# Half the columns in a triangular inverse, and a key norm moved beside the value tiles

## The reference, cut to what matters

```python
qkv = silu(causal_dwconv(concat([q, k, v]), conv_w))
q = l2norm(to_chunks(q)) * D ** -0.5
k = l2norm(to_chunks(k))
...
k_beta = k * beta[..., None]
lower = where(strict, einsum('bhncd,bhnsd->bhncs', k_beta, k) * decay, 0.0)
rhs = concatenate([v * beta[..., None], k_beta * exp(g)[..., None]], axis=-1)
sol = triangular_solve(lower, rhs, left_side=True, lower=True, unit_diagonal=True)
...
# then a scan over chunks: v_new, o_i, state
```

## Time and profile before

| | |
|---|---|
| median of 3 runs | 3832.85 us (3829.78 to 3834.25) |
| the profiled execution | 3828.58 us, span 3826.8 us |
| granted TensorE clock, mean | 0.949 |
| PE busy | 3475.4 us, 91% of the span |
| DVE / ACT / POOL busy | 47% / 34% / 11% |
| matmul L3373, L3385, L3390 | 960, 768 and 960 records |

### The profile page before, as it was taken

The page is one execution under the profiler, slowest core; times in us unless marked ns, Lnnn a source line. Parts: engine busy times, 40 slices in busy tenths (PEclk is TensorE's granted clock), DMA queues, the critical chain, the costliest instruction groups (busy, mean ns, idle before and its releaser), DMA issues. The chain is left out here.

```text
span 3826.8 us, 46458 instructions
## 1 busy us (share of the span) xinstructions
PE 3475.4 (91%) x19317; PEld 2705.3 (71%) x19317; DVE 1780.1 (47%) x2762; ACT 1308.2 (34%) x2038; POOL 420.6 (11%) x351
## 2 busy tenths in 40 slices
PE   5989897999999789998897988999989988899998
PEld 4877765788777567886665756788766665577886
DVE  4775465443332534332544454444444444554534
ACT  2332353223232332322422353333333134533333
POOL 0001000120000101100023000221001310013100
PEclk7999998999999899999899999999989989999999
DMA  6651215333221032331301103232122020213231
GB/s 228 199 175 45 78 34 187 118 124 110 90 75 55 1 132 69 105 109 35 99 18 27 37 1 110 87 100 101 66 76 61 2 63 1 88 55 110 77 110 50
DMA packets 230575, 316.69 MB, mean 83 GB/s; under 512 B 13133, under 2 KB 167606, under 8 KB 229086
## 3 DMA queue, kind: packets, MB, share of 16 engines
q1 hardware_dynamic: 230366, 313.72, 24.9%
HBM read 311.04 MB, written 6.85 MB: 83 GB/s over the span
## 5 line engine op out<-in xcount | busy, mean ns | idle before, releaser
L493 PE MATMUL out<-h_lo,w_hi 128*128 128x512 f32 x2608 | 1043.1, 400 | 52.1 <-DVE w_lo L484 47.8
L494 PE MATMUL out<-h_hi,w_hi 128*128 128x512 f32 x2608 | 1022.2, 392 | 0.0
L495 PE MATMUL out<-h_hi,w_lo 128*128 128x512 f32 x2608 | 1021.6, 392 | 0.0
L484 DVE TENSOR_TENSOR w_lo<-ring,w_hi 128x1024 fp32r<-128x1024 f32 (+2 forms) x459 | 560.7, 1227 | 980.0 <-ACT w_hi L479 974.9
L479 ACT ACTIVATE w_hi<-ring 128x1024 fp32r<-128x1024 f32 (+2 forms) x459 | 469.2, 1027 | 1152.9 <-PE out L495 1061.1
L493 PEld LDWEIGHTS out<-h_lo,w_hi 128*128 128x128 f32 x2608 | 494.0, 189 | 178.1 <-issue 60.4
L494 PEld LDWEIGHTS out<-h_hi,w_hi 128*128 128x128 f32 x2608 | 493.8, 189 | 111.9 <-issue 11.0
L495 PEld LDWEIGHTS out<-h_hi,w_lo 128*128 128x128 f32 x2608 | 493.6, 189 | 103.9
L493 PE MATMUL item_banks<-h_lo,w_hi 128*128 128x512 f32 (+1 forms) x632 | 289.4, 458 | 14.3 <-DVE w_lo L484 5.1
L494 PE MATMUL item_banks<-h_hi,w_hi 128*128 128x512 f32 (+1 forms) x632 | 255.1, 404 | 0.0
L495 PE MATMUL item_banks<-h_hi,w_lo 128*128 128x512 f32 (+1 forms) x632 | 254.8, 403 | 0.0
(11 more groups left out here) (499 smaller groups left out, 4635.8 us busy)
## 6 DMA issues: line engine op xcount, KB each, us to landing
ring<-in_mlp_w SPq DMA_DIRECT2D x30, 2048.0 KB, 8.5
ring<-in_w_up SPq DMA_DIRECT2D x44, 1024.0 KB, 7.4
tiles<-in_mod_w SPq DMA_DIRECT2D x80, 512.0 KB, 4.6
ring<-in_e_w_in SPq DMA_DIRECT2D x48, 512.0 KB, 4.1
ring<-in_w_down SPq DMA_DIRECT2D x10, 2048.0 KB, 7.7
ring<-in_w_in SPq DMA_DIRECT2D x16, 1024.0 KB, 5.2
ring<-in_o_w_in SPq DMA_DIRECT2D x7, 2048.0 KB, 7.9
tiles<-in_mod_w SPq DMA_DIRECT2D x8, 1024.0 KB, 8.8
```

Of the source, the lines that this page charges most:

```text
L484: return nc.vector.tensor_tensor(lo.bitcast(F32R), x, hi, ALU.subtract)
L493: nc.tensor.matmul(out, wh, xl, start=start, stop=False, **kw)
L494: nc.tensor.matmul(out, wh, xh, start=False, stop=False, **kw)
L495: return nc.tensor.matmul(out, wl, xh, start=False, stop=stop, **kw)
```

## The change

**Inverse.** At level n the multiplies L3373, L3385 and L3390 take as moving operand only the columns that the level changes, 32 for each head in place of 64, read in runs of 2<<n (2, 4, 8, 16, 32) columns with as many skipped. The number of matmuls and their stationary operands stay (64x64 each). ACT copies 128x96 in place of 128x192 and writes them in such runs; DVE subtracts 128x192 in place of 128x384 (last level 128x96 in place of 128x192). The copy of each level gets a tile of its own (`y_levels`, 128x1920) that POOL clears once at the start of the lane, since half of its columns are never written and serve as zeros in the stationary operand. To make room, the tiles `sb_q`, `sb_k` and `sb_v` are allocated in the attention region that uses them.

**Order.** The key norm begins at plan 67.9, 3.5 after the last key tile, and is 15.5 long, so that it stands beside the three value tiles. The SiLUs of the value tiles move behind it (plan 84.2, 84.9, 85.6), which keeps the key norm's activation tables loaded. `DELTA` becomes 87.5. Since an item that begins at or after `DELTA` is 9.4 long, item 15 is now one of those; items end at plan 167.6 in place of 163.8, and the rotary lane begins 3.8 later.

```diff
@@ delta_lane
-    v_beta, k_beta, k_end, q_run, run, attn_t, y_sb = pieces(0, 7)
+    v_beta, k_beta, k_end, q_run, run, attn_t = pieces(0, 6)
+    y_sb = [y_levels[:, n, :] for n in range(LEVELS)]
+    HALF = T * HD // 2
+    def part_of(x, n, side):
+        return x.rearrange("p (q two j) -> p q two j", two=2, j=2 << n)[:, :, side, :]
+    def inverses(n, b):
+        size = 2 << n
+        both = scratch(9, 2, 2 * size).rearrange("p (w s) -> p w s", w=2)[:, :, b * T * HD:(b + 1) * T * HD]
+        return both.rearrange("p w (q two j) -> p w q two j", two=2, j=size)[:, :, :, 0, :]
         nc.gpsimd.memset(state[:, :, :], 0.0).then_inc(zeroed, 1)
+        nc.gpsimd.memset(y_levels[:, :, :], 0.0).then_inc(zeroed, 1)
-        pe.wait_ge(zeroed, 1)
+        pe.wait_ge(zeroed, 2)
-                            last = nc.tensor.matmul((B0, B1)[b][at, t * HD:(t + 1) * HD], of_head(parts[n], b, t)[at, :],
-                                                    of_head(inv, b, t)[at, :], start=True, stop=True)
+                            last = nc.tensor.matmul((B0, B1)[b][at, t * HD // 2:(t + 1) * HD // 2], of_head(parts[n], b, t)[at, :],
+                                                    part_of(of_head(inv, b, t)[at, :], n, 0), start=True, stop=True)
-                                nc.tensor.matmul((B2, B3)[b][at, t * HD:(t + 1) * HD], of_head(inv_t, b, t)[at, :], of_head(y_sb, b, t)[at, :],
-                                                 start=True, stop=True)
+                                nc.tensor.matmul((B2, B3)[b][at, t * HD // 2:(t + 1) * HD // 2], of_head(inv_t, b, t)[at, :],
+                                                 part_of(of_head(y_sb[n], b, t)[at, :], n, 0), start=True, stop=True)
-                            last = nc.tensor.matmul((B2, B3)[b][at, (T + t) * HD:(T + t + 1) * HD], of_head(y_sb, b, t)[at, :],
-                                                    of_head(inv_t, b, t)[at, :], start=True, stop=True)
+                            last = nc.tensor.matmul((B2, B3)[b][at, HALF + t * HD // 2:HALF + (t + 1) * HD // 2], of_head(y_sb[n], b, t)[at, :],
+                                                    part_of(of_head(inv_t, b, t)[at, :], n, 1), start=True, stop=True)
-                    nc.scalar.activation(y_sb[:, b * T * HD:(b + 1) * T * HD], (B0, B1)[b][:, 0:T * HD], ACT.Copy).then_inc(y_out, 1)
+                    nc.scalar.activation(part_of(y_sb[n][:, b * T * HD:(b + 1) * T * HD], n, 0),
+                                         (B0, B1)[b][:, 0:HALF].rearrange("p (q j) -> p q j", j=2 << n), ACT.Copy).then_inc(y_out, 1)
-                        nc.vector.tensor_tensor(here, here, (B2, B3)[b][:, 0:N].rearrange("p (w n) -> p w n", w=2), ALU.subtract).then_inc(inv_done, 1)
+                        here = inverses(n, b)
+                        change = (B2, B3)[b][:, 0:2 * HALF].rearrange("p (w q j) -> p w q j", w=2, j=2 << n)
+                        nc.vector.tensor_tensor(here, here, change, ALU.subtract).then_inc(inv_done, 1)
@@ items_lane, scalar
-                steps += [(end, 2, m), (end + 3.0, 3, m)]
+                steps += [(end, 2, m), (end + 3.0 if item.silu_at is None else item.silu_at, 3, m)]
@@ second_mixer
-        BEGIN, DELTA, ROUND = 18.0, 94.0, 28.0
+        BEGIN, DELTA, ROUND = 18.0, 87.5, 28.0
+        keys_end, conv_end = (items[TC + n * GDN_T - 1].begin + items[TC + n * GDN_T - 1].length for n in (2, 3))
+        for t in range(GDN_T):
+            items[TC + 2 * GDN_T + t].silu_at = conv_end + 3.0 + 0.7 * t
-            normed = key_norm_lane(k, r, r.lane(conv_end + 3.5, 9.0),
+            normed = key_norm_lane(k, r, r.lane(keys_end + 3.5, 15.5),
```

More of the change, by code:

```diff
@@ L626, in __init__ @@
         self.chunks, self.scale, self.tile, self.func, self.moving, self.ready, self.each = chunks, scale, tile, func, moving, ready, each
-        self.begin, self.length = 0.0, 0.0
+        self.begin, self.length, self.silu_at = 0.0, 0.0, None
 def left(freed, m):
@@ L3052, in head_norm_lane, with attention_region @@
     return gate_done
-def attention_region(k, a, l, tiles, nq, kc2, vc2, ks2, kw2, vs_rows, vw_rows, gates, sq, sk, sv_rows, gz, mixT):
+def attention_region(k, a, l, tiles, nq, kc2, vc2, ks2, kw2, vs_rows, vw_rows, gates, gz, mixT):
     nc = k.nc
@@ L3068, in attention_region @@
         kc_dup, vc_rows = r.sbuf("kc_dup", [P, 2 * N_CMP]), r.sbuf("vc_rows", [P, 2, HD])
+        sq, sk, sv_rows = r.sbuf("sb_q", [P, SB_T, S]), r.sbuf("sb_k", [P, SB_T, S]), r.sbuf("sb_v", [P, TC, N_SB * HD])
         ranges = [[(W_SQ + t * P, P)] for t in range(2 * SB_T)] + [[(W_SV + t * P, P)] for t in range(2)]
@@ L3465, in _ @@
                         act.wait_ge(t_done, c * 2 * LEVELS)
-                    nc.scalar.activation(y_sb[:, b * T * HD:(b + 1) * T * HD], (B0, B1)[b][:, 0:T * HD], ACT.Copy).then_inc(y_out, 1)
+                    if n == 0 and b == 0 and c == 0:
+                        act.wait_ge(zeroed, 2)
+                    nc.scalar.activation(part_of(y_sb[n][:, b * T * HD:(b + 1) * T * HD], n, 0),
+                                         (B0, B1)[b][:, 0:HALF].rearrange("p (q j) -> p q j", j=2 << n), ACT.Copy).then_inc(y_out, 1)
             yield t0 + 21.0
@@ L3522, in _ @@
                     if n < LEVELS - 1:
-                        here = invs.rearrange("p (w b n) -> p w b n", w=2, b=2)[:, :, b, :]
-                        nc.vector.tensor_tensor(here, here, (B2, B3)[b][:, 0:N].rearrange("p (w n) -> p w n", w=2), ALU.subtract).then_inc(inv_done, 1)
-                    else:
-                        here = inv_t[:, b * half:(b + 1) * half]
-                        nc.vector.tensor_tensor(here, here, (B2, B3)[b][:, half:N], ALU.subtract).then_inc(inv_done, 1)
+                        here = inverses(n, b)
+                        change = (B2, B3)[b][:, 0:2 * HALF].rearrange("p (w q j) -> p w q j", w=2, j=2 << n)
+                        nc.vector.tensor_tensor(here, here, change, ALU.subtract).then_inc(inv_done, 1)
+                    else:
+                        here = part_of(inv_t[:, b * half:(b + 1) * half], n, 1)
+                        change = (B2, B3)[b][:, HALF:2 * HALF].rearrange("p (q j) -> p q j", j=2 << n)
+                        nc.vector.tensor_tensor(here, here, change, ALU.subtract).then_inc(inv_done, 1)
             for i in range(2):
@@ L3653, in second_mixer, with scratch @@
             item_banks, stat_banks, delta_banks = r.psum("item_banks", [P, 2, S]), r.psum("stat_banks", [P, 2, S]), r.psum("delta_banks", [P, 4, S])
-            def scratch(first, count=1):
+            def scratch(first, count=1, more=0):
                 width = N_GDN * HD
                 if first < 11:
-                    return scratch_own[:, first * width:(first + count) * width]
+                    return scratch_own[:, first * width:(first + count) * width + more]
                 return scratch_mix[:, (first - 11) * width:(first - 11 + count) * width]
@@ L3691, in second_mixer @@
                                          stat_banks[:, 1, :], freed)
-            conv_end = items[12].begin + items[12].length
-            normed = key_norm_lane(k, r, r.lane(conv_end + 3.5, 9.0),
+            normed = key_norm_lane(k, r, r.lane(keys_end + 3.5, 15.5),
                                    [(qkv[:, t, :], HD ** -0.5 if t < GDN_T else 1.0) for t in range(2 * GDN_T)], silu_done,
                                    kv_turned[:, 0:2, :], kv_turned[:, 2:4, :], stat_banks)
-            delta_lane(k, r, r.lane(DELTA, 1.0), qkv, g, beta, beta_eg, to_end, mixT, scratch, state, delta_banks, steps_ready, normed, silu_done,
+            delta_lane(k, r, r.lane(DELTA, 1.0), qkv, g, beta, beta_eg, to_end, mixT, scratch, y_levels, state, delta_banks, steps_ready, normed, silu_done,
                        ROUND)
@@ L3699, in second_mixer @@
                         [kc2, vc2, ks2, kw2], kv_turned[:, 0:2, :], stat_banks, [(freed[0], (last_kv + 1) // 2), (freed[1], last_kv // 2)], [(normed, 2 * GDN_T)])
-        attention_region(k, a, l, tiles, nq, kc2, vc2, ks2, kw2, vs_rows, vw_rows, gates, sq, sk, sv_rows, gz, mixT)
+        attention_region(k, a, l, tiles, nq, kc2, vc2, ks2, kw2, vs_rows, vw_rows, gates, gz, mixT)
 def first_part_of(tiles):
```

6 lines of the change are left out of this document (3 added, 3 removed).

## The result

The changed kernel takes 3894.86 us (median of 4 runs, 3892.77 to 3902.84) against 3833.09 for the kernel before. The ratio is 1.017, with a 95% interval of 1.0158 to 1.0182: 62 us slower. The forecast was 3828, its range ended at 3842, and the slower rival stood at 3845.

What follows compares the result with a forecast made beforehand. PE was taken to set the pace. A pass was 38.6 + 170.4 - 2.5 = 206.5 us against 210.5 and 207.4, together 4.9 less: 3823.7 for the profiled execution, 3828 as median; range 3809 to 3842.

Steps and rivals of the forecast that it cites:

- the slower rival: Longer waits in key norm and round 1 prologue keep the clock low twice as long: 3845 us, chance 0.17.
- PE, half the moving columns: 0 us: Inverse levels: weight loads set the pitch, so a group of twelve stays 0.35 to 0.36 us and nothing is gained.
- Rounds: 170.4: Four rounds of a pass, with items pushed in (+3.7): 45.1 + 45.5 + 41.3 + 38.5 = 170.4 us.
- The first rival: Inverse levels: PE's groups follow the columns and halve, 39 + 5 us less, 3789 us; chance 0.07.
- Rival 3: Key norm and prologues of rounds 1 and 4: clock stays low twice as long, 8.5 us a pass, 3845; chance 0.17.
- Its deciding point: The slower clock outcome decides once PE's waits beside the value tiles pass some 10 us a pass.
- ACT and DVE, 2.5 us a pass: Inverse levels: halved copy and subtraction 0.08 and 0.20 us shorter each, mostly hidden, saving 2.5 us a pass.
- nine starts and two subtractions: Rounds 1 to 3: starts right behind the copy and last-level subtractions save 0.1 us each, 1.3 together.
- Key norm stretch, 38.6: Item 10 step f5 to round 1: PE work 25.5, waits 8.4, clock loss 4.7; 42.0 (40.5) becomes 38.6 us.
- POOL's clearing: Start of the lane: clearing 128x1920 costs 0 as POOL is idle; 2.6 us a pass if not covered.
- the table loads: Value SiLUs behind the key norm: two more loads, 1.28 us each, hidden; 2.6 us a pass if not.

Runs made afterwards that it cites:

- e3: The changed kernel with PE multiplying all 64 columns for each head again, ACT and DVE still halved: 3832.7 us, ratio 1.0002.
- e1: The kernel before with only the changed order (key norm, value SiLUs, DELTA 87.5), the inverse with all 64 columns: 3839.9 us, ratio 1.0017.
- e4: The kernel before with only ACT's copy and DVE's subtraction halved, PE's columns and the order as before: 3825.4 us, ratio 0.9985.
- e6: e4 plus nine unread 128x128 float32 matmuls on PE in front of the prologue's wait in rounds 1, 2 and 4: 3811.9 us, ratio 0.9943.
- e11: The kernel before with only nine unread matmuls added in front of the waits of rounds 1, 2 and 4: 3825.2 us, ratio 0.9985.
- e14: e3 plus twelve unread 128x128 matmuls in front of the prologue's wait in rounds 1, 2 and 4: 3825.7 us, ratio 0.9984.
- e9: The whole changed kernel plus twelve unread 128x128 matmuls in front of the prologue's wait in rounds 1, 2 and 4: 3857.1 us, ratio 1.0068.
- e12: e6 plus unread matmuls in three more waits (three and fifteen in the key norm, eight before round 1): 3811.9 us, ratio 0.9955.
- e2: The changed kernel with the old order put back, so only the half-column inverse on PE, ACT and DVE: 3890.7 us, ratio 1.0156.
- e13: The whole changed kernel plus sixteen unread matmuls in the waits of rounds 1 and 2 and fourteen in round 4: 3849.5 us, ratio 1.0048.
- e16: e12 with half the columns on PE: 3827.1 us, ratio 0.9991.
- e10: e2 plus nine unread matmuls in rounds 1, 2 and 4, behind the wait, after the first level's first group: 3840.1 us, ratio 1.0022.

## Why the prediction was wrong

**The step that failed** is "PE, half the moving columns: 0 us". As a statement on the groups' length it held: 0.35 us for twelve records, 0.89 for 24, at 2.4 GHz. But I priced the edit only by the length of its own instructions, and took the clock as a thing that waits alone decide. The term of the sum that it broke is "Rounds: 170.4", which measured 209.0 us in the first pass and 200.3 in the second. e3 against the changed kernel puts 62 us on PE's columns. The time lies in the stretches at 1.2 GHz: 199 us of low clock against 48, and half of the difference of 151 is 76, of which part falls on waits that are there anyway. Round 3, which had no fall, is as long as in e3 (41.6 and 41.9). The first rival, groups that follow the columns, is ruled out by the same rows.

**Rival 3** named the right place (a fall at the prologue's wait) and the right sign, but the wrong cause: it had the longer waits of the new order lengthen the stretches twofold. e1 has those waits of 3.6 us with all columns, and its stretches are 3.4 and 6.8 us. Its deciding point, waits of some 10 us beside the value tiles, was not met (6.7 in the first pass). Its price of 8.5 us a pass was too small by about four times, since it went by the old trace, where no fall in the levels was longer than 6.8 us.

**ACT and DVE, 2.5 us a pass.** Sizes right (252 and 353 ns), and nearly at full rate in runs of two columns: such copies take 256 to 259 ns, the others some 251. The forecast was 5.0 us in the two passes; the sums give 3.5 (e4 against before), 2.6 (e3 against e1) and 5.0 (e6 against e11, with the waits filled), the medians of e4 7.4 (interval 2.3 to 9.2). Right in the main. Its parts were added wrongly: nine starts and two subtractions at 0.1 us are 1.1 and not 1.3, which changes nothing in the forecast.

**Key norm stretch, 38.6.** Measured 35.5 and 35.7. The waits were 0.91, 2.04 and 3.71, 6.7 in place of 8.4, and the clock fell once, for 6.8 us, a loss of 3.4 in place of 4.7. PE's own work of 25.5 fits: 25.5 + 6.7 + 3.4 = 35.6. The waits in sum are those of the old order; the gain is the nine steps that went into the rounds.

**Rounds, 170.4.** With all columns and a steady clock they are 170.3 (e14), term by term 46.0, 44.7, 41.9 and 37.7 against 45.1, 45.5, 41.3 and 38.5. That the sum agrees to 0.1 us is luck: terms off by up to 0.9 cancel, and e14 has the waits of rounds 1, 2 and 4 filled. At the clock as it was, e3 has 174.1: round 1 gets the 3.4 us that rival 3 gave it. The waits of PE for that DVE step are now, against the earlier trace rows,

```profile
PE delta_banks L3385 <- DVE delta_scratch L3524: 11.0, 4, 3.6
```

I had put that at 3.0 and let it cost nothing in the forecast. The order costs 6.4 us in the two passes (e1) where I had about 0. Round 1 is 3.4 us a pass above its term, round 4 grew by 4.9 where I had 3.5, rounds 2 and 3 are 0.6 above theirs, and the shorter key norm stretch gives back 3 us a pass. POOL's clearing (1.7 us) and the table loads stayed hidden: no wait of PE for either.

**What stays open.** By what measure the chip judges PE's work is not shown. Whether it is the number of moving columns or their being read in runs is not either, since every halved multiply has both. That a mix of 10 or 18 halved groups does no harm and 28 do, and that the same wait of 0.94 us tipped it in one pass of e9 and not in the other, is what there is. Each account of the clock rests on one profiled execution of a kernel, with two passes in it. The swing of 3403 to 3420 us in the unchanged remainder was not traced.

## What to carry to other kernels

An edit that makes small matmuls smaller, where their pace doesn't follow their columns (0.35 us a group with 64 and with 32), saves nothing on PE and can cost the clock; halve what ACT and DVE touch and leave PE's columns. When a prediction rests on "busy as before", ask whether the clock in that stretch rests on work that the edit removes. And look for waits of 1 to 4 us in front of sparse stretches of PE: nine matmuls whose result nobody reads, in each of three waits, gained 13 us of 3825 here (e6; 9.8 by the two passes), at 0.9943 of the time before, with e12 the fastest kernel of the study.

## What the runs showed of the hardware that was not expected

PE busy 27.00 of 27.00 us at a granted clock of 0.50 (e2). Twenty-eight half-width groups a round, 64x64 weights with 32 moving columns, stay at 1.2 GHz for 24 to 41 us once there (10 in one round of the changed kernel; 51 in e2's round 4, some 17 of them behind the round), where the same groups with 64 columns leave it after 3 to 7. Half-width groups also fall to it where the same groups with 64 columns don't: 2.3 us behind a wait of 2.46 us (e2, twice), behind 1.63 us (e13, twice), and once with no wait over 0.16 us in the 9.9 us before (e16). Nine float32 matmuls of 128x128 end the state (e10, round 2), at 3.84 us for the nine against 2.17 at 2.4 GHz.
